# Sparse softmax in steps of a head pair and a query tile

## What is computed

```python
score = einsum('bqh,bqhk->bqk', iw * IDX_HEADS**-0.5, relu(iq . ixk * IDX_DIM**-0.5))
score = where(key <= query, score, -inf)
_, sel = top_k(score, 128)                       # per query, one choice for all heads
logits = einsum('bqhd,bqkd->bqhk', q, k[sel]) * dh**-0.5 + rel_bias[bucket(pos_q - pos_k)]
p = softmax(where(valid, logits, -inf))          # 8 heads of width 64, one shared k and v
y_c = einsum('bqhk,bqkd->bqhd', p, v[sel])
```

## Time and profile before

| | us |
|---|---|
| median of 3 runs | 1426.58 |
| lowest, highest | 1406.52, 1429.9 |
| the profiled execution | 1419.21 |
| its span | 1417.5 |

### The profile page before, as it was taken

The page is one execution under the profiler, slowest core; times in us unless marked ns, Lnnn a source line. Parts: engine busy times, 40 slices in busy tenths (PEclk is TensorE's granted clock), DMA queues, the critical chain, the costliest instruction groups (busy, mean ns, idle before and its releaser), DMA issues.

```text
span 1417.5 us, 17812 instructions
## 1 busy us (share of the span) xinstructions
PE 1327.0 (94%) x6538; PEld 988.4 (70%) x6538; DVE 775.8 (55%) x1582; ACT 608.2 (43%) x1130; POOL 181.8 (13%) x302
## 2 busy tenths in 40 slices
PE   3589999889999999999999999988999999999998
PEld 2278766645557888888878876655555788888887
DVE  7856677767643334454446577677844233335442
ACT  3335556666563223233333455566645322323330
POOL 3400212123330000000000021112333000000000
PEclk9899999999999999999999999999979999999999
DMA  6432112100240322223231311210014033222331
GB/s 163 127 97 89 60 61 45 31 30 2 75 134 31 119 89 89 90 89 119 89 90 60 106 44 60 45 46 15 25 51 132 32 98 110 90 89 89 110 98 60
DMA packets 118423, 109.14 MB, mean 77 GB/s; under 512 B 34496, under 2 KB 101056, under 8 KB 118336
## 3 DMA queue, kind: packets, MB, share of 16 engines
q1 hardware_dynamic: 110096, 107.96, 25.3%
q10 hardware_dynamic: 8240, 0.03, 0.3%
HBM read 100.64 MB, written 7.34 MB: 76 GB/s over the span
## 4 chain that ended last, share of the span: by engine, by line
PE 78%; DVE 10%; ACT 5%; issue 3%; POOL 2%; SPq 1%; DMA 0%; ACTq 0%; DVEq 0%; POOLq 0%
PE bank L722 20%; PE bank L724 19%; PE bank L723 19%; PE bank L1020 4%; PE bank L988 3%; PE bank L829 2%; PE bank L1002 2%; PE bank L981 2%; DVE w_lo L631 2%; PE bank L853 1%; POOL reach L457 1%; PE bank L843 1%; PE bank L990 1%; DVE score L1600 1%; ACT w_hi L625 1%
## 5 line engine op out<-in xcount | busy, mean ns | idle before, releaser
L722 PE MATMUL bank<-h_hi,w_hi 128*128 128x512 f32 (+1 forms) x928 | 362.8, 391 | 10.2 <-DVE ds_q L1609 5.7
L723 PE MATMUL bank<-h_lo,w_hi 128*128 128x512 f32 (+1 forms) x928 | 354.3, 382 | 0.0
L724 PE MATMUL bank<-h_hi,w_lo 128*128 128x512 f32 (+1 forms) x928 | 354.3, 382 | 0.0
L631 DVE TENSOR_TENSOR w_lo<-raw,w_hi 128x2048 fp32r<-128x2048 f32 (+2 forms) x98 | 188.1, 1919 | 142.5 <-ACT w_hi L625 142.2
L722 PEld LDWEIGHTS bank<-h_hi,w_hi 128*128 128x128 f32 x928 | 176.5, 190 | 54.4 <-issue 8.5
L625 ACT CAST w_hi<-raw 128x2048 fp32r<-128x2048 f32 (+2 forms) x100 | 159.4, 1594 | 120.3 <-PE bank L724 120.3
L723 PEld LDWEIGHTS bank<-h_lo,w_hi 128*128 128x128 f32 x928 | 176.7, 190 | 33.9 <-issue 2.9
L724 PEld LDWEIGHTS bank<-h_hi,w_lo 128*128 128x128 f32 x928 | 176.7, 190 | 33.7
L1406 ACT ACTIVATE gate<-bank,gains 128x512 f32<-128x512 f32 x48 | 33.0, 688 | 166.1 <-PE bank L724 166.1
L1892 POOL TENSOR_SCALAR probs<-probs,stat 128x128 f32<-128x128 f32 (+3 forms) x128 | 74.5, 582 | 181.1 <-DVE stat L1711 175.4
L722 PE MATMUL bank<-br_hi,w_hi 128*128 128x512 f32 x192 | 74.7, 389 | 0.0
(11 more groups left out here) (218 smaller groups left out, 2327.3 us busy)
## 6 DMA issues: line engine op xcount, KB each, us to landing
raw<-in_w_in SPq DMA_DIRECT2D x56, 1024.0 KB, 5.2
raw<-in_w_branch SPq DMA_DIRECT2D x12, 1024.0 KB, 5.2
raw<-in_w_out SPq DMA_DIRECT2D x8, 1024.0 KB, 5.1
bias<-bias_dram SPq DMA_DIRECT2D x16, 256.0 KB, 2.9
bias<-bias_dram SPq DMA_DIRECT2D x16, 192.0 KB, 2.6
x_sb<-in_x SPq DMA_DIRECT2D x4, 512.0 KB, 4.9
bias_dram<-bias_out SPq DMA_DIRECT2D x8, 256.0 KB, 2.9
raw<-in_w_in SPq DMA_DIRECT2D x4, 512.0 KB, 4.6
```

The source lines that it names most:

```text
L631: e.tensor_tensor(w_lo[:, s % RING, a:b], raw[:, s % RAW, a:b], w_hi[:, s % RING, a:b].bitcast(F32), ALU.subtract).then_inc(*lo_signal(nam ...
L722: pe.matmul(out_ap, lh, rh, start=start and i == 0, stop=False)
L723: pe.matmul(out_ap, lh, rl, start=False, stop=False)
L724: mm = pe.matmul(out_ap, ll, rh, start=False, stop=stop and i == n - 1)
```

## The change

The sparse part leaves the common loop. It now runs in 16 steps, each a pair of heads and one query tile: two units, `dsa_units(j)`, ordered pair, tile, head. In a step TensorE does both scores, then both masks (`chosen_of`), then what is left of the dense part, then the transposes of step j-2 (`DSA_T`), then the values of step j-3 (`DSA_AV`). Scores use four banks, 0 to 3. The copies have four buffers of their own (`probs_dsa`). ScalarE does both exponentials, then both copies of step j-2, then from step 7 on every fourth step the pair's result, then a half of a weight split. VectorE does both bias additions, the leftover dense copies, both inverses, and a half of a split. Each bias strip has its own semaphore and is loaded when the same strip's buffer was used up, four steps before. The first gate tile z0_0 is computed in two halves, in TensorE's steps 16 and 17, where only transposes and values are left. In the dense part, ScalarE now squares the next head's k before the t=0 exponential.

```diff
-SPLIT_Z = {N_SOFT // 2 + 6: ("z0_0", 0), N_SOFT // 2 + 10: ("z0_0", 1),
-           N_SOFT // 2 + 12: ("z0_1", 0), N_SOFT // 2 + 14: ("z0_1", 1)}
+N_MLA = N_SOFT // 2
+DSA_STEPS = N_MLA // 2
+DSA_T, DSA_AV = 2, 3
+SPLIT_Z = {3: ("z0_0", 0), 5: ("z0_0", 1), 7: ("z0_1", 0), 9: ("z0_1", 1)}
...
+        def dsa_units(j):
+            return [(N_MLA + 2 * j + o, o, 2 * (j // ST) + o, j % ST) for o in range(2)]
...
+                for j in range(DSA_STEPS):
+                    for u, o, h, t in dsa_units(j):
+                        if j >= ST:
+                            e.wait_ge(*row_max.at(u - 2 * ST))
+                        e.dma_start(bias[:, o, OFF[t]:OFF[t] + P * (t + 1)], bias_dram[h, t * P:(t + 1) * P, 0:P * (t + 1)]
+                                    ).then_inc(*bias_in[o][t].tick(h, by=16))
...
         def s_bank(u):
-            return bank[2 + u % S_RING]
+            return bank[2 + u % S_RING] if u < N_MLA else bank[(u - N_MLA) % 4]
...
+            if br == "dsa":
+                return probs_dsa[:, u % 4, 0:w]
...
+            if br == "dsa":
+                return u - 4 if u >= N_MLA + 4 else N_MLA - 1
...
+                    if u >= N_MLA + 4:
+                        pe.wait_ge(*row_max.at(u - 4))
+                    elif u >= N_MLA:
+                        pe.wait_ge(*probs_exp.at(N_MLA - 1 if u % 2 else N_MLA - 2))
...
+                def values_of(j):
+                    for u, o, h, t in dsa_units(j):
+                        pe.wait_ge(*turned_copied(u))
+                        if t == 0 and o == 0:
+                            pe.wait_ge(*(y_out["dsa"].at(h // 2 - 1) if h else y_out["mla"].at(3)))
...
+                for j in range(DSA_STEPS + DSA_AV):
+                    if j < DSA_STEPS:
+                        for u, o, h, t in dsa_units(j):
+                            s_of(u)
+                        for u, o, h, t in dsa_units(j):
+                            chosen_of(u)
+                    for i in (N_MLA + 2 * j, N_MLA + 2 * j + 1):
+                        mla_tail(i)
+                    if 0 <= j - DSA_STEPS < 2:
+                        if j == DSA_STEPS:
+                            use("z0_0")
+                            pe.wait_ge(*row_max.at(N_SOFT - 3))
+                        mm = project("z0_0", "z0_0", 0, P, part=j - DSA_STEPS)
+                        if j > DSA_STEPS:
+                            mm.then_inc(*dense.tick("z0_0"))
+                    if 0 <= j - DSA_T < DSA_STEPS:
+                        for u, o, h, t in dsa_units(j - DSA_T):
+                            t_of(u)
+                    if 0 <= j - DSA_AV < DSA_STEPS:
+                        values_of(j - DSA_AV)
...
+                    if t == 0 and h + 1 < HEADS:
+                        sq_k(h + 1)
+                    exp_of(i)
...
+                for j in range(DSA_STEPS + DSA_AV + 1):
+                    if j < DSA_STEPS:
+                        for u, o, h, t in dsa_units(j):
+                            exp_of(u)
+                    if N_MLA + 2 * j - AV_LAG == N_MLA - 1 or N_MLA + 2 * j + 1 - AV_LAG == N_MLA - 1:
+                        pair_out("mla", 3, N_MLA - 1)
+                    if 0 <= j - DSA_T < DSA_STEPS:
+                        for u, o, h, t in dsa_units(j - DSA_T):
+                            e.wait_ge(*probs_turned.at(u))
+                            e.wait_ge(*pv_done.at("soft", turned_before(u)))
+                            e.copy(turned(u), t_bank(u)[:, 0:P * (t + 1)]).then_inc(*probs_t_ready["dsa"].tick(u))
+                    if j >= DSA_AV + ST and (j - DSA_AV) % ST == 0:
+                        pair = (j - DSA_AV) // ST - 1
+                        pair_out("dsa", pair, N_MLA + 8 * pair + 7)
+                    if j in SPLIT_Z:
+                        split_hi(e, *SPLIT_Z[j])
...
+                for j in range(DSA_STEPS):
+                    for u, o, h, t in dsa_units(j):
...
+                        e.wait_ge(*logits.at(u))
+                        e.wait_ge(*probs_exp.at(u - 4))
+                        e.wait_ge(*bias_in[o][t].at(h))
+                        e.wait_ge(*probs_turned.at(u - PR))
...
+                    for i in (N_MLA + 2 * j, N_MLA + 2 * j + 1):
+                        if i - T_LAG < N_MLA:
+                            turned_mla(i - T_LAG)
+                    for u, o, h, t in dsa_units(j):
+                        inverse(u)
+                    if j - 1 in SPLIT_Z:
+                        split_lo(e, *SPLIT_Z[j - 1])
```

More of the change, by code:

```diff
@@ L378, in build @@
         probs_t_ready = {br: signal(f"probs_t_ready_{br}") for br in ("mla", "dsa")}
-        bias_in = [signal(f"bias_in{i}") for i in range(2)]
+        bias_in = [[signal(f"bias_in{o}_{t}") for t in range(ST)] for o in range(2)]
         gate_sig = signal("gate_sig")
@@ new lines, in mla_tail @@
+                def mla_tail(i):
+                    if i - T_LAG < N_MLA:
+                        t_of(i - T_LAG)
+                    if i - AV_LAG < N_MLA and soft_units[i - AV_LAG][1] % 2:
+                        av_of(i - AV_LAG)
+                for i in range(N_MLA):
+                    s_of(i)
+                    if i < 2:
+                        if i == 0:
+                            pe.wait_ge(*y_out["stick"].at(3))
+                        values_b(2 * i)
+                        values_b(2 * i + 1)
+                    br, h, t = soft_units[i]
+                    if h + 1 < HEADS:
+                        if t == 0:
+                            prep_k(h + 1)
+                        if t == 2 and h + 2 < HEADS:
+                            prep_q(h + 2)
+                    if i >= T_LAG:
+                        t_of(i - T_LAG)
+                    if h + 1 < HEADS:
@@ L1053, in _ @@
                     for m in range(4):
+                        if n == 0 and m == 0:
+                            continue
                         if m % 2 == 0:
@@ new lines, in pair_out @@
+                def pair_out(br, pair, u):
+                    e.wait_ge(*pv_done.at("soft", u))
+                    e.copy(y[:, 4 + pair, :] if br == "mla" else y_dsa[:, pair, :], bank[Y][:, :]).then_inc(*y_out[br].tick(pair))
+                for i in range(N_MLA):
+                    if i > AV_LAG and (i - AV_LAG - 1) % 8 == 7:
+                        pair_out("mla", (i - AV_LAG - 1) // 8, i - AV_LAG - 1)
+                    br, h, t = soft_units[i]
+                    if t == 0 and h + 1 < HEADS:
+                        sq_k(h + 1)
+                    exp_of(i)
+                    if i < 2:
+                        for s in (2 * i, 2 * i + 1):
+                            e.wait_ge(*dense.at(f"v_b{s}"))
+                            e.copy(v_b[:, s, :], t_bank(s)[:, :]).then_inc(*act_evac.tick(f"v_b{s}"))
+                    if h + 1 < HEADS:
+                        if i == 0:
+                            rs_q(1)
+                        if t == 1:
+                            rs_k(h + 1)
+                        if t == 2 and h + 2 < HEADS:
+                            sq_q(h + 2)
+                        if t == 3 and h + 2 < HEADS:
+                            rs_q(h + 2)
@@ new lines, in turned_mla @@
+                def turned_mla(u):
+                    w = P * (soft_units[u][2] + 1)
+                    e.wait_ge(*probs_turned.at(u))
+                    if turned_before(u) is not None:
+                        e.wait_ge(*pv_done.at("soft", turned_before(u)))
+                    e.tensor_copy(turned(u), t_bank(u)[:, 0:w]).then_inc(*probs_t_ready["mla"].tick(u))
+                for i in range(N_MLA):
+                    br, h, t = soft_units[i]
+                    w = P * (t + 1)
+                    negated = stat[:, 16 + i % 4:17 + i % 4]
+                    e.wait_ge(*logits.at(i))
+                    if i >= 4:
+                        e.wait_ge(*probs_exp.at(i - 4))
+                    e.tensor_reduce(negated, s_bank(i)[:, 0:w], AX_X, ALU.max, negate=True).then_inc(*row_max.tick(i))
+                    if i:
@@ L1753, in _ @@
[L1753 to L1755 removed]
+                                        ).then_inc(*topk.tick("chosen", tt))
+                    if i >= T_LAG:
+                        turned_mla(i - T_LAG)
+                    if h + 1 < HEADS:
                         if t == (0 if h else 1):
```

149 lines of the change are left out of this document (39 added, 110 removed).

## The result

| | before | changed |
|---|---|---|
| median of 20 executions, us | 1426.58 | 1417.86 |
| lowest, highest, us | 1401.09, 1432.28 | 1413.43, 1423.61 |
| profiled execution, us | 1419.21 | 1423.61 |
| its span, us | 1417.5 | 1421.9 |

The ratio, changed to before, is 1.0077 with a 95% interval from 1.0054 to 1.01: 0.8% slower. The executions of the kernel before fall into groups by their granted clock, and the ratio is taken against the group with the high one; the plain medians stand the other way, 0.6% apart. The forecast was 1425.0, about no change. The number is 7 us high, but it hides two things: the changed kernel is slower than before is at a high clock, and faster than before usually is.

A forecast was written before the change was run, and what follows sets the result against it. It took TensorE's order of work as the bound, with a ring of waits pacing the new sparse steps: 1419.2 - 14.6 (stretches) - 2.8 (square) = 1402, + 23 for low clock = 1425 us; range 1392 to 1460.

The forecast's parts named there:

- TensorE's work: Sparse steps: a pair of scores costs one score, a step falls from 3.2 to 2.4 us, saving 13 us a layer.
- The ring: Sparse steps: transposes, bias additions, exponentials and copies wait on each other in a loop, 2.90 us a step against 2.4 of TensorE work.
- the copy-out wait: Sparse values wait for ScalarE to copy the pair's result out of its bank: 3.9 us, at three places a layer.
- C(0) to C(13): From the end of step 0's first-unit transposes to step 13's: 43.2 us at full clock, plus 2.0 for the weight split.
- Rival 3: TensorE sets the pace of the sparse stretch, 2.4 us a step with no loop of waits: 1380 us; chance 0.12.
- Square: Dense softmax: squaring the next head's k before the t=0 exponential saves 1.4 us a layer, 2.8 in all.
- strips: Bias strips: the same 32 DMAs, each due four steps (12 us) after its buffer is free; transfers never waited for.
- tile: Gate tile z0_0 costs the same wherever it is computed, 5.5 us.
- The +2.0 for the split: Weight-split halves on VectorE, 1.23 us, behind the reciprocals of steps 4, 6, 8 and 10, add 2.0 us a stretch.
- The low clock of the new order: Sparse stretches: 35 us at 1.2 GHz in each, a third of it lost, 23 us in all.
- Rival 2: Sparse stretches at the low clock nearly throughout, with the loop of waits: 1460 us; chance 0.2.
- Rival 1: Loop of waits, but clock low under 10 us a stretch, since paired scores fill the array: 1402 to 1408; chance 0.15.

The follow-up runs named there:

- e4: Changed kernel with ScalarE's turn reordered: the pair's result first, then both copies, then both exponentials; 1377.98 us, ratio 0.979.
- e1: Kernel before with one edit alone: ScalarE squares the next head's k ahead of the t=0 exponential; 1401.75 us, ratio 0.995.
- e2: Changed kernel with ScalarE's copies of step j-2 ahead of the exponentials of step j; 1404.78 us, ratio 0.9976.
- e3: Changed kernel with the copy of the pair's result first in ScalarE's turn, the rest unaltered; 1400.67 us, ratio 0.9967.
- e7: e4 with z0_0 computed behind the last values, as in the kernel before; 1376.93 us.
- e6: e4 with each mask directly behind its unit's scores, so that no two scores stand side by side; 1389.8 us, ratio 0.985.
- e14: Kernel before with ScalarE's copy ahead of its turn's exponential and all four weight-split halves in t=0 turns; 1394.79, 1395.18, 1396.59 and 1417.09 us, ratio 0.982.
- e5: Changed kernel with each mask directly behind its unit's scores, so that no two scores stand side by side; 1453.01 us, ratio 1.030.

## Why the prediction was right where it was, and wrong

**TensorE's work: right.** A pair costs one score (1.13 us for four passes); some 12 us a layer were saved, by e4's busy time against e1's. The prediction's own terms give 16x0.73 = 11.7; its 13 comes from rounding 3.2 and 2.4.

**The ring and the copy-out wait: there, and in sum as large as forecast.** 3.3 us for a step with t=0, against 3.36; the other steps were sized at 2.90 and take 3.03 behind t=3 and 3.7 to 3.8 at the start. The misses nearly cancel: C(0) to C(13) takes 51.5 us in the first layer with 17 of them low, an estimated 44 to 45 at full clock, where the sum has 43.2 + 2.0. The wait at the values is 3.98 us in the first layer and up to 4.3 in the second, three times in each, against 3.9. e2 and e3 take one each away and the time falls by 13 and 17 us; e4 takes both and it falls by 40. Together they are worth 10 us more than the two singly; part of it is that e2 and e3 each keep some of the low clock (14 to 17 us a stretch), and e4 none. Rival 3's 1380 was about the time of the kernel without them. What the Trainium skill gives for a dimension of up to 64 ("TensorEngine Tiling (Array Packing)", Theoretical Speedup: up to 2x) holds for the scores, 1.13 us for two where one takes 1.12, and the kernel's time shows it once the waits are gone.

**Square, strips, tile: right.** -1.4 us in each dense stretch; VectorE never waits for a strip; moving z0_0 does not change the time (e7). The +2.0 for the split was not measured by itself.

**The low clock of the new order: right in kind, too large.** I took 35 us a stretch at a third; it is 23.8, since a spell behind a copy-out lasted 6.8 and not 10 us, and each us seems to cost more than a third: (71.0 to 72.1 - 62.4) / 23.8 = 0.36 to 0.41, if 62.4 is right for the full clock, which no run shows. So 9 to 10 us a stretch instead of 11.7. With 9.5 the sum gives 1402 + 19 = 1421; measured 1417.9. The granted clock of the stretch was to be under 0.8 and is 0.85. Rival 2, low nearly throughout, did not come. The rule of the Trainium skill on HAM oscillation ("TensorE: Matmul & The Clock Gate") holds here: the clock falls at each of the three stalls of 4 us, and the round behind it begins at 1.2 GHz. That the stretch would then be low throughout was my reading of it, and did not come: the granted clock is back at 2.4 GHz after 6.8 us, before the next stall.

**The step that failed: what the new time was held against.** The sum subtracts "139.4 together" from the profiled 1419.2, and its end says "the spread from 1406.5 to 1429.9 is of the size of the clock's share, and I keep my number as it is". But 139.4 is the time of one execution. At full clock the old stretch takes 60.4 us, and the new one 62.4 in my own sum: there the change loses 4.0 us in two layers and gains 2.8 by the square, +1.2. The 14.6 us that I counted as saved were low clock of that one execution (139.4 - 120.8 = 18.6). The prediction had even worked it out, 6.7 and 13.2 us, and did not take it off before comparing. And the old order does not pay this each time: 41, 65 and 55 us low in the two stretches of three profiles, some 46 outside them (85, 106 and 109 in the whole, less these: 41 to 54), and 52 in the whole of an execution at 0.981, which by this estimate leaves about 6 for both stretches. The new order pays 2 x 23.8 each time, 19 us. There were two comparisons to make, and I made one that lies between them:

- against executions of before at 0.981: +1.2, +19, and -3 for the 6 us low of the old stretches: 17 us slower than 1404.5. Measured 13.4 (1417.9).
- against those at 0.962: +1.2 + 19 - 0.43 x 63 = 7 us faster than 1429.1. Measured 11.2.

Both sums come out 4 us above what was measured; that rest is not explained.

The three runs shown, 1406.52, 1426.58 and 1429.9, already stood in two groups, with the profiled 1419.2 in neither. They called for a comparison with each group: by these sums some 1422 us, slower than the one and faster than the other.

**Rival 1's reason**, that half-row scores are what the clock suffers from, was given and then not used for the old order: there 28 of 48 waits of about 1 us were followed by 3.4 to 58 us low, in the paired order 1 of 58, and the waits of 2 us and more by 3.4 to 6.8.

**What stays open.** Which of the short waits brings a spell: 0.93 us did in seven stretches and not in e1's second, in the same code. Why the new order hardly ever falls behind such a wait. Whether half-row scores would bring the spells back in it: e6 has only the first score's wait (1.05 us), and in the old order that one brought a spell in 5 of 14 stretches, so its two without one tell little. And why the kernel before has two groups of executions at all, and e1 never the lower one.

## What to carry over

When an in-order engine does two units a turn, put first in its turn what others wait for from earlier turns (the result bank, the copies) and last the new work that nobody needs yet: here the order of three blocks is worth 40 us, and only with it does the rewrite bring its 17. Before a stretch's time is used as a reference, divide it into full-clock and low time and look at the spread of the runs: a saving that sits in the clock of one profile is no saving. Count the waits of a stretch too and look at the granted clock behind each: in the old order of this kernel a wait of about 1 us could be followed by up to 58 us at 1.2 GHz, in the new one nearly all spells came with waits of 2 us or more.

## What the hardware showed

- TensorE stayed at 1.2 GHz for 58.0 us while it was busy for 57.00 of them (e14, first layer), and in the same kernel's other layer, in the same code, for 3.4.
- In the changed kernel each of 12 waits of 4 us was followed by a low spell, 6.8 us long in 11 cases and 3.4 in one (three copy-outs, two layers, two profiles).
- In the old order 28 of 48 waits of 0.56 to 1.42 us had a low spell behind them; in the new one with paired scores 1 of 58 of 0.91 to 1.57 us, and all 27 of 2.04 to 5.21 us.
- A microsecond at the low clock costs 0.43 us in the old order, and an estimated 0.36 to 0.41 in the new.
- One engine slows another with which it shares no data: GpSimd's normalization of 384 columns took 1.48 to 1.66 us beside VectorE's subtraction (1.2 us), and 0.59 elsewhere in the same profiles.
- Doing without the pairs added 11.7 us of score work a layer, of which 6.6 showed where the waits were gone (e6); where they stayed, the stretch grew by 15 and 19 us, low clock included (e5).
